# Cached attention of a decoder layer in two sets of four sequences, the first among the prompt's attention

## The reference, cut to what matters

```
past_k = cache_k[l][page_table].reshape(DB, n_pages * PAGE_SIZE, ATT_HEADS, HEAD_DIM)
gate = jnp.einsum('bhqd,bhnd->bhqn', qh.astype(jnp.float32), kmean)   # 4 blocks of 256 keys
_, sel = lax.top_k(gate, n_top)                                       # 3 of them, and its own
s = jnp.einsum('bhqd,bhqnkd->bhqnk', q_c, kg, preferred_element_type=jnp.float32) * scale
p = jax.nn.softmax(s, axis=-1)
o = jnp.einsum('bhqnk,bhqnkd->bhqd', p, vg.astype(jnp.float32))
```

## Time and profile before

| | us |
|---|---|
| median of 3 runs (593.17 to 600.68) | 596.73 |
| the profiled execution | 596.88 |
| its span in the trace | 594.9 |
| DVE busy in the span | 350.0 |
| PE busy in the span | 534.4 |

### The profile page before, as it was taken

One profiled execution on the slowest core, in us unless ns is written; L12 is line 12 of the kernel. 1 busy time (PEld: TensorE's weight loads), 2 busy tenths in 40 slices (PEclk: granted clock), 3 DMA queues, 4 the chain that ended last, 5 costly groups with the idle time before them and its releaser, 6 DMA issues.

```text
span 594.9 us, 10233 instructions
## 1 busy us (share of the span) xinstructions
PE 534.4 (90%) x3943; PEld 450.2 (76%) x3943; DVE 350.0 (59%) x548; ACT 163.5 (27%) x230; POOL 56.6 (10%) x126
## 2 busy tenths in 40 slices
PE   7879997997998888988789689987999999999997
PEld 5557775675688766865564059887999999999996
DVE  4540269478798787955734537465665566455441
ACT  4101010811132122211000224364343443424420
POOL 6800010000104800000101000000000000000000
PEclk8979897997699999999969899998999999999999
DMA  9996356476049467643739998595465655645201
GB/s 294 332 302 207 108 189 218 123 204 221 19 150 324 144 221 245 217 132 119 244 111 376 384 352 268 173 298 163 148 209 162 195 169 168 195 144 193 73 19 37
DMA packets 98998, 116.79 MB, mean 196 GB/s; under 512 B 6317, under 2 KB 81278, under 8 KB 98934
## 3 DMA queue, kind: packets, MB, share of 16 engines
q1 hardware_dynamic: 93218, 104.42, 54.8%
q10 hardware_dynamic: 3908, 7.42, 3.5%
q0 software_dynamic: 1824, 4.30, 2.6%
HBM read 113.30 MB, written 2.99 MB: 195 GB/s over the span
## 4 chain that ended last, share of the span: by engine, by line
PE 64%; DVE 21%; DMA 7%; ACT 3%; issue 3%; ACTq 1%; SPq 0%; DVEq 0%
PE bank L336 61%; DVE prod L916 5%; DVE s_all L1019 5%; DVE mats L916 3%; DMA ring<-in_ada_w_dram 2%; DMA ring<-in_w_out_dram 2%; DVE BTP L916 1%; DVE cv L1127 1%; DMA ring<-in_cache_v_dram 1%; DMA x_nat<-in_x_sample_dram 1%; PE bank L373 1%; PE bank L382 1%; ACT w_part L1692 1%; DMA qb<-q_rows_dram 1%; PE bank L517 1%
## 5 line engine op out<-in xcount | busy, mean ns | idle before, releaser
L336 PE MATMUL bank<-a_hi,w_part 128*128 128x264 f32 x832 | 153.5, 286 | 2.1 <-DVE a_lo L1464 2.1
L916 DVE TENSOR_TENSOR w_part<-ring,w_part 128x2048 fp32r<-128x2048 f32 (+1 forms) x38 | 84.9, 2236 | 89.2 <-ACT w_part L1692 89.2
L336 PEld LDWEIGHTS bank<-a_hi,w_part 128*128 128x128 f32 x832 | 129.8, 189 | 2.6 <-issue 2.6
L336 PE MATMUL bank<-a_lo,w_part 128*128 128x264 f32 x416 | 118.4, 285 | 0.0
L1692 ACT ACTIVATE w_part<-ring 128x2048 fp32r<-128x2048 f32 (+1 forms) x38 | 70.9, 1871 | 86.0 <-PE bank L336 75.0
L336 PE MATMUL bank<-hT,ring 128*128 128x264 f32 x352 | 85.7, 406 | 0.8 <-ACT proj L1555 0.8
L336 PEld LDWEIGHTS bank<-hT,ring 128*128 128x128 f32 x352 | 70.0, 201 | 14.9 <-issue 2.4
L336 PEld LDWEIGHTS bank<-a_lo,w_part 128*128 128x128 f32 x416 | 79.0, 190 | 0.1
L336 PE MATMUL bank<-hid_hi,w_part 128*128 128x264 f32 x352 | 64.9, 285 | 0.0
L336 PEld LDWEIGHTS bank<-ident 128*128 128x128 f32 x362 | 48.1, 212 | 10.4 <-issue 5.6
L336 PEld LDWEIGHTS bank<-hid_hi,w_part 128*128 128x128 f32 x352 | 54.5, 188 | 0.1
(11 more groups left out here) (326 smaller groups left out, 570.3 us busy)
## 6 DMA issues: line engine op xcount, KB each, us to landing
ring<-in_ada_w_dram SPq DMA_DIRECT2D x24, 1024.0 KB, 7.3
ring<-in_cache_k_dram SPq DMA_DIRECT2D x64, 256.0 KB, 3.6
ring<-in_w_in_dram SPq DMA_DIRECT2D x11, 1024.0 KB, 5.6
ring<-in_w_gate_dram SPq DMA_DIRECT2D x11, 1024.0 KB, 5.3
ring<-in_w_up_dram SPq DMA_DIRECT2D x11, 1024.0 KB, 5.3
ring<-in_cache_v_dram SPq DMA_DIRECT2D x40, 256.0 KB, 4.2
ring<-in_w_down_dram SPq DMA_DIRECT2D x8, 1024.0 KB, 5.1
ring<-in_cache_v_dram ACTq DMA_DIRECT2D x24, 256.0 KB, 5.2
```

Of the source, the lines that this page charges most:

```text
L336: return pe.matmul(out, lhsT, rhs, start=start, stop=stop, skip_group_check=True)
L916: return v.tensor_tensor(out, a, b_, op)
```

## The change

Cached attention is done in two sets of four sequences. `OWN` moves ahead of the second level. A new step `G 0` (block sums, ranking, maxima of sequences 0 to 3) stands after `M 2`, `DMAX 0` and `DEXP 0` among the heads, `V 0` to `V 3` between `H 2` and `H 6`. `G 1`, `DMAX 1`, `DEXP 1` and `V 4` to `V 7` come after the last keys. The keys of sequences 4 to 7 (`K 8` to `K 15`) are later in the table, and are multiplied in two halves of 1024 columns, since the upper half of `prod` now holds the first set's probabilities. The probabilities of the four sequences of a set lie in different columns of a 32-column weight, so that their value products add up in one bank. ACT copies that bank out (`pv_rows`), and eight small products with a selector (`selq`) pick each head's columns and turn them. The masks on DVE, the eight folds, and `VE` go. SP issues all value pages. The stores of the last rows move ahead of the pooling on POOL.

```
-             "QB3 K5 GC KNORM GBC KR ROWS KK W6 K6 QB4 TI VR L1 K7 KROW W0 K8 M1 VROW L2 QB5 K9 M2 TAILS L3 S K10 M3 A4 "
-             "H0 QB6 K11 L4 M4 H1 A5 H2 L5 K12 M5 A6 QB7 H3 K13 H4 L6 K14 M6 POOL H5 UA A7 K15 H6 UB UC H7 UD A8 HE OWN "
-             "A9 DMAX DEXP V0 XA V1 XB V2 XC V3 XD V4 MX V5 V6 MW0 V7 VE MD MW1").split()
+             "K5 GC KNORM GBC KR ROWS KK W6 K6 TI VR OWN L1 K7 KROW W0 M1 VROW L2 M2 TAILS L3 G0 S M3 K8 A4 H0 DMAX0 L4 "
+             "H1 DEXP0 M4 K9 A5 H2 L5 V0 M5 H3 K10 V1 H4 L6 K11 V2 M6 POOL H5 K12 UA V3 FO0 H6 K13 UB A6 UC H7 K14 UD A7 "
+             "HE K15 A8 G1 A9 XA DMAX1 XB DEXP1 V4 XC V5 XD V6 MX MW0 V7 FO1 MD MW1").split()
...
             def page_values(q):
...
+                g, j = q // GS, q % GS
+                if j == 0:
+                    if g:
+                        keep_awake(4, 6)
+                    pe.wait_ge(sem("p_ready"), g + 1)
+                    opened(f"pv{g}", (3, 4)[g])
+                b = bank[(3, 4)[g]]
...
+            def fold(g):
+
+                if g:
+                    keep_awake(5, 6)
+                pe.wait_ge(sem("pv_rows"), g + 1)
+                b = opened(f"yT{g}", (3, 7)[g])
                 for c in range(AC):
-                    last = pe.transpose(b[:, c * P:(c + 1) * P], w_a[:, c * P:(c + 1) * P], ident[:, :])
-                closed(last, "yT8")
+                    for h2 in range(2):
+                        r = 64 * h2
+                        last = mm(b[r:r + 64, c * GS:(c + 1) * GS], stg[:, g, c * P + r:c * P + r + 64], selq[:, 2 * c + h2, :])
...
+            def k_item_low(q, hf):
...
+                half = PGI // 2
+                for w in range(2):
+                    ins = tt(prod[:, 0:1024].rearrange("p (k n) -> p k n", k=half),
+                             slot[:, 1024 * w:1024 * w + 1024].rearrange("p (k n) -> p k n", k=half),
+                             bc(qb[:, q % 2:q % 2 + 1, :], [P, half, AW]), ALU.mult)
...
+            def group_gates(g):
+                v.wait_ge(sem("tails_out"), 64)
...
-            g.wait_ge(sem("max_diag"), 1)
-            step(g.memset(prod[:, :], 0.0))
+            g.wait_ge(sem("k_scored"), NS)
+            step(g.memset(prod[:, 0:1024], 0.0))
             g.sem_inc(sem("p_zeroed"), 1)
...
-                    load_pages(sp, it, range(PGI // 2 if kind == "v" and i[0] >= 2 else PGI))
+                    load_pages(sp, it, range(PGI))
```

More of the change, by code:

```diff
@@ L711, in own_scores @@
             def own_scores():
-                keep_awake(6, 8)
                 pe.wait_ge(sem("own_diag"), 1)
-                b = opened("own", 6)
+                b = opened("own", 3)
                 closed(mm(b[:, 0:NS * H], ones[0:NS, :], own8[:, 1, :]), "own")
[L716 to L721, removed]
@@ L747, in page_values, with group_sums @@
[L747 to L751 removed]
+            def group_sums(g):
+                if g:
+                    keep_awake(6, 8)
+                pe.wait_ge(sem("k_scored"), GS * (g + 1))
+                b = opened(f"gsT{g}", (3, 6)[g])
+                mm(b[:, 0:GW], ones[:, :], s_all[:, g * GW:(g + 1) * GW])
+                for n in range(2):
+                    o = g * GW + n * P
+                    last = pe.transpose(b[:, GW + n * P:GW + (n + 1) * P], s_all[:, o:o + P], ident[:, :])
+                closed(last, f"gsT{g}")
@@ new lines, in denominators @@
+            def denominators(g):
+                e = w_b[:, g * GW:(g + 1) * GW]
+                sm3, sm4, sm5 = (sm64[:, n, g * GS:(g + 1) * GS, :] for n in range(3, 6))
+                v.wait_ge(sem("exp8"), g + 1)
+                inc(tt(paged(e), paged(e), bc(flat(gate4, g).unsqueeze(2), [P, GS * NB, PPB, H]), ALU.mult), "exps")
+                v.wait_ge(sem("exps"), g + 1)
+                b = full(v, f"den{g}")
+                freed(v.tensor_reduce(sm4, queried(b[:, 0:GW]).rearrange("p q n h -> p q h n"), AX, ALU.add), f"den{g}")
+                v.wait_ge(bank_free[filled[f"den{g}"][0]], frees_at(f"den{g}"))
+                step(tt(sm4, sm4, sm3, ALU.add))
+                step(v.reciprocal(sm4, sm4))
+                tt(sm5, sm3, sm4, ALU.mult)
+                v.wait_ge(sem("p_zeroed"), g + 1)
+                for j in range(GS):
+                    last = tt(pP[g][:, j * NPG:(j + 1) * NPG, j * H:(j + 1) * H], queried(e)[:, j, :, :],
+                              bc(sm4[:, j:j + 1, :], [P, NPG, H]), ALU.mult)
+                inc(last, "p_ready")
@@ new lines, in fold @@
+            def fold(g):
+                own_v = w_b[:, g * GW:g * GW + AC * GS].rearrange("p (c q) -> p c q", c=AC)
+                cols = slice(T + g * GS, T + (g + 1) * GS)
+                v.wait_ge(sem("p_ready"), g + 1)
+                for h2 in range(2):
+                    r = slice(64 * h2, 64 * h2 + 64)
+                    last = tt(own_v[r, :, :], proj[r, VC0:VC0 + AC, cols],
+                              sm64[r, 5, g * GS:(g + 1) * GS, :].rearrange("p q (c w) -> p w c q", w=2)[:, h2, :, :], ALU.mult)
+                step(last)
+                b = full(v, f"yT{g}")
+                freed(tt(mixT[:, PCH:PCH + AC, cols], b[:, 0:AC * GS].rearrange("p (c q) -> p c q", c=AC), own_v, ALU.add),
+                      f"yT{g}")
+                v.wait_ge(bank_free[filled[f"yT{g}"][0]], frees_at(f"yT{g}"))
+                if g:
+                    v.sem_inc(sem("mix"), 1)
```

242 lines of the change are left out of this document (104 added, 138 removed).

## The result

The changed kernel takes **606.16 us** (median of four runs, 602.86 to 609.80) against 598.33 us for the kernel before beside it (593.17 to 600.68): ratio 1.013, 95% interval 1.007 to 1.019. A second set of runs of the same text gave 607.4 us and 1.014 (1.008 to 1.020). The forecast was 587.2 us in a range of 576 to 600. It is missed on the far side: the change costs a little over 1%.

What follows compares the result with a forecast made beforehand. DVE was taken as nearly full to 284 us, then the cached-softmax chain, then DMA at 349 GB/s. Later last keys (-31.6), part two (+16.0) and part three (+25.6) gain 10.0 us, less 0.3 for the clock: 587.2 us, range 576 to 600.

Steps and rivals of the forecast that it cites:

- part two: From the last keys to the second set's first value product: 21.0 us where it was 37.0, 16.0 us gained.
- part three: From the second set's first value product to the output projection: 23.2 us where it was 48.8, 25.6 gained.
- The work up to the last keys: DVE's work from `K 7`, starting at 173.5, to the last keys: 105.4 us, so they can't end before 278.9.
- The first level: DVE's wait for the projection slot on PE, now behind `OWN`, which `K 8` used to cover: 5.0 us.
- The second: DVE's wait at the second level, six products behind the first, which `K 9` used to cover: 1.9 us.
- The stores of the last rows: DVE idle before `G 0` until these stores land at 202.0: 7.6 us, with 5.7 us to landing.
- The fifth level: DVE's wait there for `V 0`, 1.9 us on PE: 3.1 us, between 0 and 5.
- The rest 4.8 us: DVE's remaining waits before the last keys: PE's sums in `DEXP 0`, the pool, the pair `A 7`, the last head.
- Part one: Up to the last keys: DVE's work plus 22.4 us of waits, ending at 301.3, 31.6 us later than before.
- rival 3: Value transfers stay the bound after the softmax, if the first set's pages come late: 596 us; chance 0.05.
- Rival 1: DVE's waits up to the last keys mostly filled: 576 us if half of 22.4 us go; chance 0.33.
- Rival 2: PE's clock falls to about 0.75 from 200 to 300 us: +11 us a level, two give 609; chance 0.09.

Runs made afterwards that it cites:

- a_fixed: Changed kernel with each slot of pages loaded by one transfer from fixed pages, without table reads: 600.0 us, ratio 1.005 to the kernel before.
- a_fk: Changed kernel with one fixed-page transfer a slot and no table reads, and `K 8`, `K 9` back in their old places: 596.7 us, ratio 0.996 to the kernel before.
- f_both: `a_best` without filler matmuls at heads 0 to 2 and without the nine ahead of the second set's maxima: 588.9 us, ratio 0.982 to the kernel before.
- a_best: Changed kernel with `K 8`, `K 9` in old places, some page numbers read early, and pooling held back: 597.9 us, ratio 0.996 to the kernel before.
- D: Theory that DVE lost the keys covering its waits; changed kernel with `K 8`, `K 9` back in old places: 601.7 us, ratio 1.006 to the kernel before.
- P: Theory that POOL's pooling slows `G 0`; changed kernel with the pooling held back behind it: 604.2 us, ratio 1.007 to the kernel before.
- a_nod: Changed kernel without the filler matmuls at heads 1 to 7: 602.9 us, ratio 1.005 to the kernel before.
- Q: Theory that the queue engine's own work, 4.3 us a slot of pages, is the bound; tested on the changed kernel by `a_fixed`: 600.0 us.
- a_f1: Changed kernel with no other edit than removing the filler matmuls at heads 0 to 2: 608.2 us, ratio 1.014 to the kernel before.
- f_early: `a_best` without the filler matmuls at heads 0 to 2: 591.0 us, ratio 0.985 to the kernel before.

## Why the prediction was wrong, by its own steps

From the forecast's 587.2 to the profiled 602.86 there are 15.7 us: last keys +11.1, part two +0.3, part three +4.1, the rest of the kernel +0.6, less the 0.3 that the sum had for the clock and 0.2 around the span. The median of the four runs lies another 3.3 higher.

- **The work up to the last keys was right.** `K 7` starts at 173.0 (forecast 173.5), and of the 139.4 us to 312.4 DVE waits 33.0 and works 106.4 (105.4). That holds only as a sum: `G 0` took 7.6 us for 5.0.
- **The first level** waited 7.7 us (5.0). `W 0` began on PE at 177.0, behind `own`, for which PE had waited 2.6 us, and products that took 3.64 us for 16 where two lots of 8 take 2.1 later on: after that wait the granted clock was 0.53 from 172.6 to 176.1, and the forecast had no half clock there. **The second** waited 2.2 (1.9).
- **The stores of the last rows:** 4.6 us (7.6). They landed sooner; see below. This error was in the kernel's favour.
- **The fifth level** 4.5 us (3.1).
- **"The rest 4.8 us" is the step that failed.** It came to 14.0: 33.0 less the four above. It was taken from the holes of the old order, as if the engines behind DVE had nothing new to do. The changed order gives one queue engine ten slots of pages from 239 to 282 us, 43 us of work without a break, and gives PE the first set's sums and products. Part one has no term for either. "SP issues all four pages of each" stands only in part three, where the last of three slots was put at 13 us. The queue engine is not all of it: with its work gone (`a_fixed`) the same rest is still about 11 us, and 44.7% of its chain is PE's products. What brought the last keys forward was the cures together: all waits are 26.2 us in `a_fk` and 20.5 in `f_both`, against the 22.4 of the forecast.
- **What part one missed of the queue engine** is in the sentence in rival 3 that each page "is asked for when the item five places ahead is released". It is asked for when SP gets to it. SP waited 34.0 us, from 184 to 219, for `K 8` to be multiplied, which now stood later, and then had everything to do at once. The average of 130 to 230 GB/s left room on the transfers, and none on the engine that starts them.
- **Part two was right:** 21.3 us (21.0), in part by luck. The ranking began 3.0 us after the last keys and not 1.2, and the clock of 0.50 that the sum allowed for was 0.92.
- **Part three:** 27.3 us (23.2). The last value slot's products began 16 us after the first, not 13. The chain ran over SP to the output weights, which landed at 353.7, and not over the norm. With the table reads gone (`a_fixed`) the part was 24.4 us.
- **Rival 1** (filled waits) went the other way. **Rival 2** (clock) had its condition at 0.75; it was 0.95 from 184 to 284. Its arithmetic of one level, 11.5 us on PE beside 11.6 on DVE, held a truth that I did not use: with loads so equal each engine waits for the other without a low clock. In `a_best` PE was busy 32.1 of the 34 us from 213 to 247, at 0.90, while DVE was busy 21.2. **Rival 3** had a part of the right place and the wrong reason.
- **The signs.** "The DMA share of the tail is clearly under 1" failed (0.98), and the output projection started 48.7 us after the last keys, not 44.

What stays open: how the 33 us of waits divide among the causes in one and the same execution, since a cure moves waits as well as removing them, how much of D's gain is SP's earlier release, and what P and the fillers of the later heads (`a_nod`, 0.8%) are worth by themselves. The loss against the kernel before is accounted for: with Q and D cured it is gone.

## What to carry to other kernels

Cost a transfer twice, once for its bytes and once for the engine that starts it; when loads are moved into a stretch, add up that engine's starts and table reads there, and look for a long wait in its order behind which they all pile up. Where two or three engines are each nearly full in strict order, a cure of one may show little or nothing (`a_f1`) and the same cure much when the others are cured (`f_early`), so try cures together before a theory is dropped. Filler matmuls were set for an order of work; when the order changes, set them anew.

## What the runs showed of the hardware

- A page of 256 KB whose number is read from a table costs its starting engine 1.07 us: 0.51 for the start and about 0.55 for the read. The transfers themselves reached 357 GB/s from 284 to 312 us, pages and weight slots together, and 349 in the value stretch of the kernel before.
- The same four stores of the last rows land in very different times. Instructions on the tile `w_ab`, time to landing, of the changed kernel, where DMA moved 15 GB/s from 197 to 202 us:

```profile
DMA to landing us min/median/max: 1.6/1.9/2.9
```

and of `a_best`, where it moved 369 GB/s from 201 to 206.3 us:

```profile
DMA to landing us min/median/max: 5.0/5.2/5.3
```

  The page "DMA: Bandwidth & Descriptors" of the Trainium skill (anatomy of a DMA on the GpSimd path) has 2.0 us for a small one. The first trace agrees with it, the second and the earlier trace rows with 5.7 do not.
- Three of DVE's four additions of two tiles in `G 0` took 0.58 to 0.76 us beside POOL's work, the fourth 0.31; in `G 1`, without it, each took 0.29. The reductions took 0.42 both times. The page "SBUF — State Buffer" of the Trainium skill (two separate sides) says that a DVE operation with two SBUF inputs and a GpSimd operation that reads SBUF can't hold one pair of ports at the same time, and that the one that starts second waits. By that rule the additions and not the reductions are held up, and the trace agrees. An operation on one tile and a number (L1374) was held up as well, 0.70 us against 0.23, which two inputs don't explain.
